# Expert biases as one-pass bf16 products in three parts, and expert 30's gate and up weights in single pieces

## The reference, cut to what matters

```
logits = xt @ router_w + router_b            # top 4 of 32, softmax gates
for each expert e, over its rows xb:
    gu  = xb @ w_gate_up[e] + b_gate_up[e]   # 1024 x 2048, bias 2048
    g, u = min(gu[:, :1024], 7), clip(gu[:, 1024:], -7, 7)
    act = (u + 1) * g * sigmoid(1.702 * g)
    y  += gate * (act @ w_down[e] + b_down[e])   # 1024 x 1024, bias 1024
```

## Time and profile before

| what | value |
|---|---|
| three runs | 1134.79, 1135.81 and 1138.35 us |
| the profiled execution: its time | 1133.35 us |
| the profiled execution: its span | 1131.5 us |
| mean granted clock of TensorE | 0.989 |
| read from HBM | 430.56 MB, 381 GB/s over the span |
| busy TensorE, DVE, ACT, GpSimd | 1089.5, 273.1, 156.6, 8.2 us |

### The profile page before, as it was taken

The page is one execution under the profiler, slowest core; times in us unless marked ns, Lnnn a source line. Parts: engine busy times, 40 slices in busy tenths (PEclk is TensorE's granted clock), DMA queues, the critical chain, the costliest instruction groups (busy, mean ns, idle before and its releaser), DMA issues.

```text
span 1131.5 us, 15121 instructions
## 1 busy us (share of the span) xinstructions
PE 1089.5 (96%) x6391; PEld 482.1 (43%) x6391; DVE 273.1 (24%) x701; ACT 156.6 (14%) x326; POOL 8.2 (1%) x20
## 2 busy tenths in 40 slices
PE   8999999999999899998999989999899998999997
PEld 6788885633333333333333333333233332333332
DVE  1698742551111111111111111111011110111111
ACT  3453341400000000000000000000000000010011
POOL 1000000000000000000000000000000000000000
PEclk9999999999999999999999989999899999999999
DMA  9933289699999999999999999999999999999994
GB/s 285 333 106 114 78 289 372 241 428 428 429 429 430 425 429 429 430 430 427 430 431 430 429 429 432 431 428 429 427 431 431 429 426 428 431 430 428 425 426 185
DMA packets 46231, 432.72 MB, mean 382 GB/s; under 512 B 4244, under 2 KB 23007, under 8 KB 28367
## 3 DMA queue, kind: packets, MB, share of 16 engines
q1 hardware_dynamic: 45472, 431.03, 91.4%
q0 software_dynamic: 320, 0.43, 0.2%
q10 hardware_dynamic: 366, 0.15, 0.1%
HBM read 430.56 MB, written 1.05 MB: 381 GB/s over the span
## 4 chain that ended last, share of the span: by engine, by line
PE 88%; DMA 7%; issue 2%; DVE 1%; ACT 1%; SPq 0%; DVEq 0%; ACTq 0%
PE psum L872 37%; PE psum L908 19%; DMA arena<-in_w_gate_up 7%; PE psum L668 5%; PE psum L918 5%; PE psum L841 4%; PE psum L578 4%; PE psum L893 3%; PE psum L861 3%; PE psum L716 2%; PE psum L743 2%; PE psum L887 1%; PE psum L850 1%; PE psum L659 1%; PE psum L619 0%
## 5 line engine op out<-in xcount | busy, mean ns | idle before, releaser
L872 PE MATMUL psum<-arena 128*64 128x512 f32 x2048 | 457.4, 605 | 26.5 <-issue 22.3
L872 PEld LDWEIGHTS psum<-arena 128*64 128x64 f32 x2048 | 146.5, 139 | 332.4 <-issue 324.8
L908 PE MATMUL psum<-arena 128*64 128x512 f32 x1024 | 227.0, 596 | 0.0
L1510 DVE TENSOR_SCALAR arena<-psum 128x512 f32<-128x512 f32 x32 | 22.1, 691 | 737.9 <-PE psum L872 733.7
L908 PEld LDWEIGHTS psum<-arena 128*64 128x64 f32 x1024 | 70.7, 137 | 153.8 <-issue 153.8
L1189 ACT COPY arena<-psum 128x256 f32<-128x256 f32 x32 | 11.9, 372 | 546.0 <-PE psum L850 546.0
L918 PE MATMUL psum<-arena 64*128 64x512 f32 x256 | 63.6, 615 | 0.7 <-ACT arena L1202 0.7
L668 PE MATMUL psum<-arena 128*128 128x256 f32 x256 | 59.0, 381 | 0.3 <-ACT arena L1085 0.3
L1202 ACT COPY arena<-psum 128x512 f32<-128x512 f32 x32 | 18.7, 585 | 271.7 <-PE psum L908 271.7
L668 PEld LDWEIGHTS psum<-arena 128*128 128x128 f32 x256 | 47.8, 190 | 7.3 <-ACT arena L1085 0.5
L841 PE MATMUL psum<-arena 128*128 128x64 bf16 x1488 | 48.4, 193 | 2.2
(11 more groups left out here) (222 smaller groups left out, 537.6 us busy)
## 6 DMA issues: line engine op xcount, KB each, us to landing
arena<-in_w_gate_up SPq DMA_DIRECT2D x56, 4096.0 KB, 29.2
arena<-in_w_down SPq DMA_DIRECT2D x63, 2048.0 KB, 26.3
arena<-in_w_gate_up SPq DMA_DIRECT2D x16, 2048.0 KB, 12.8
arena<-in_w_in SPq DMA_DIRECT2D x9, 1024.0 KB, 6.2
arena<-in_w_in SPq DMA_DIRECT2D x8, 512.0 KB, 8.2
arena<-in_w_out SPq DMA_DIRECT2D x2, 2048.0 KB, 14.0
arena<-in_x SPq DMA_DIRECT2D x4, 512.0 KB, 16.9
arena<-in_w_o_mla SPq DMA_DIRECT2D x1, 2048.0 KB, 11.4
```

What stands on the lines that cost most here:

```text
L872: last = mm(b[64 * half:64 * half + 64, :], xe[i][:, k, :], slot_gu[slot][:, j, o + half * 512:o + half * 512 + 512], start=(k == 0 and fi ...
L908: last = mm(b[64 * c:64 * c + 64, :], aT[:, j, 64 * h:64 * h + 64], slot_dn[slot][:, j, c * 512:(c + 1) * 512], start=False, stop=(h == DC ...
L1510: ts(g_s, G, LIMIT, None, ALU.min).then_inc(S.g_ready, 1)
```

## The change

The biases are stored as three bf16 parts whose sum is the float32 value: the rounded value, the rounded rest, and the rest of that. The three parts lie on three groups of 32 partitions (`PARTS` = 96), `pick` becomes a bf16 matrix that repeats the selection in each group, and one bf16 matmul over 96 partitions gives the selected bias. `biases` and `down_bias` become 4 and 2 such matmuls.

SP loads b_gate_up and b_down three times, on the three groups, into `staged`, which lies in the place of ring slot 3, when all gate columns are done; these six DMAs stand ahead of w_out. GpSimd makes the parts in 15 steps (`bias_step`): three copies to bf16 on 96 partitions, then twice three subtractions and three copies, on 64 and on 32 partitions. Piece 3, which goes into the slot of `staged`, is loaded after pieces 4 to 7 and after the 15th step. TensorE waits for that step before expert 0's biases; DVE waits only for the norm's weight.

Expert 30's gate and up pieces are no longer paired: four DMAs of 2 MB, and TensorE waits for each. For this TensorE's last round of five experts is written out behind a loop of five rounds. DVE's `hot` moves to another tile.

```diff
 E = 32
+BIAS_STEPS = 15
 TOPK = 4
...
 def in_pairs(n, c):
-    return c < GC and 2 < n < E - 1
+    return c < GC and 2 < n < E - 2
 def loads_of():
...
         at += D
-        biasgu = words(at, FF); at += FF
+        bias_gu = words(at, FF).bitcast(BF16); at += FF
         ov_s = words(at, 320)
...
         ph = [half_words(at), half_words(WB + 5120), half_words(at + 64)]; at += 128
-        pick = [words(at, 64), words(WB + 5184, 64), rwt[:, 0:2, :].rearrange("p k e -> p (k e)"),
-                rwt[:, 2:4, :].rearrange("p k e -> p (k e)"), words(at + 64, 64)]; at += 128
+        pick = [words(at + 32 * i, 32).bitcast(BF16) for i in range(ROUND - 1)] + [words(WB + 5184, 32).bitcast(BF16)]; at += 128
         xe = [grid(at, KD, SLOTS), grid(WB + 5504, KD, SLOTS), grid(at + 512, KD, SLOTS)]; at += 1024
...
         router_bias = tk[:, 384:384 + E]
+        bias_dn = [words(W0 + C_MASK, 256).bitcast(BF16), tk[:, 128:384].bitcast(BF16)]
+        PARTS = 3 * E
+        staged = words(slot_at[3], 3 * D)
         xn3 = words(WB, 3072).bitcast(BF16).rearrange("p (t s d) -> p t s d", t=2, s=3)
...
         in_wqb, in_wkvb, in_wo, in_pw2 = sem("in_wqb"), sem("in_wkvb"), sem("in_wo"), sem("in_pw2")
+        in_norm = sem("in_norm")
         in_wout, in_res, in_router, in_bias = sem("in_wout"), sem("in_res"), sem("in_router"), sem("in_bias")
...
                      "router_ready logits_ready bound_ready exp_done mask_ready rank_ready place_ready "
-                     "hi_ready remains_ready mid_ready split_ready cnt_ready gate_ready overflow_ready used built gathered "
+                     "hi_ready remains_ready mid_ready split_ready cnt_ready gate_ready overflow_ready bias_step used built gathered "
                      "xe_half xe_ready turned sT_ready g_ready a_step sg_ready act_ready aT_done aT_ready y_ready scattered0 scattered "
...
             load_piece(1)
+            sp.wait_ge(*piece_used["g", 7])
+            for i in range(3):
+                sp.dma_start(staged[E * i:E * (i + 1), 0:2 * FF], a["b_gate_up"][0]).then_inc(in_bias, 16)
+                sp.dma_start(staged[E * i:E * (i + 1), 2 * FF:3 * FF], a["b_down"][0]).then_inc(in_bias, 16)
             sp.wait_ge(S.oT_ready, 4)
...
             sp.dma_start(router_bias, a["router_b"][0].partition_broadcast(P)).then_inc(in_router, 16)
-            for k in (2, 3):
-                load_piece(k)
+            load_piece(2)
             sp.wait_ge(S.ymix_ready, 4)
...
                 load_piece(k)
+            sp.wait_ge(S.bias_step, BIAS_STEPS)
+            load_piece(3)
             for k in (8, 9):
...
             pool.wait_ge(S.oT_ready, 4)
-            for o in range(2):
-                pool.dma_start(biasgu[E * o:E * (o + 1), :], a["b_gate_up"][0][:, FF * o:FF * (o + 1)]
-                               ).then_inc(in_bias, 16)
-                pool.dma_start(biasgu[E * (2 + o):E * (3 + o), 0:512], a["b_down"][0][:, 512 * o:512 * (o + 1)]
-                               ).then_inc(in_bias, 16)
             with nc.allow_non_contiguous_dma(reason="the norm's weight in the order of the experts' rows"):
                 pool.dma_start(fnw.rearrange("p (c j) -> p c j", j=4),
-                               a["ffn_norm_w"][0].rearrange("(c p j) -> p c j", c=2, j=4)).then_inc(in_bias, 16)
+                               a["ffn_norm_w"][0].rearrange("(c p j) -> p c j", c=2, j=4)).then_inc(in_norm, 16)
+
+            pool.wait_ge(in_bias, 16 * 6)
+            parts = [(bias_gu, 0, 2 * FF), (bias_dn[0], 2 * FF, 512), (bias_dn[1], 2 * FF + 512, 512)]
+            done = 0
+            for level in range(3):
+                rows_in = slice(0, E * (3 - level))
+                for to, at, n in parts:
+                    y = staged[rows_in, at:at + n]
+                    if level:
+                        nc.gpsimd.tensor_tensor(y, y, to[rows_in, :], ALU.subtract).then_inc(S.bias_step, 1)
+                        done += 1
+                if level:
+                    pool.wait_ge(S.bias_step, done)
+                for to, at, n in parts:
+                    nc.gpsimd.tensor_copy(to[rows_in, :], staged[rows_in, at:at + n]).then_inc(S.bias_step, 1)
+                    done += 1
+                pool.wait_ge(S.bias_step, done)
+            assert done == BIAS_STEPS
         @block.tensor
...
                     for o, b in ((0, G), (1, U)):
-                        last = mm(b[64 * half:64 * half + 64, :], pick[p][E * o:E * (o + 1), :],
-                                  biasgu[E * o:E * (o + 1), half * 512:half * 512 + 512], start=first, stop=not first)
+                        at = o * FF + half * 512
+                        last = mm(b[64 * half:64 * half + 64, :], pick[p][0:PARTS, :], bias_gu[0:PARTS, at:at + 512],
+                                  start=first, stop=not first)
                 return last
...
                 for c in range(2):
-                    rows_of = slice(E * (2 + c), E * (3 + c))
-                    mm(b[64 * c:64 * c + 64, :], pick[p][rows_of, :], biasgu[rows_of, 0:512], start=True, stop=False)
+                    mm(b[64 * c:64 * c + 64, :], pick[p][0:PARTS, :], bias_dn[c][0:PARTS, :], start=True, stop=False)
             def down(n, p, pieces, halves=range(DC), b=Y, in_pieces=False):
...
                     pe.wait_ge(S.built, 1)
-                    pe.wait_ge(in_bias, 80)
+                    pe.wait_ge(S.bias_step, BIAS_STEPS)
                     last = biases(0, ROUND - 1, False)
...
             biases(1, 0, True)
-            with pe.Fori(0, (E - 2) // ROUND) as it:
+
+            def expert(n, u, gu, dn):
+                after = SIDE[(u + 1) % ROUND]
+                gate_up(n, SIDE[u], gu)
+                turn(n, SIDE[u])
+                turn_act(n - 1)
+                gather(n + 1, after)
+                down(n - 1, (u - 1) % ROUND, dn)
+                biases(n + 1, (u + 1) % ROUND, True)
+                scatter(n - 1, SIDE[u - 1])
+
+            rounds = (E - 2) // ROUND
+            with pe.Fori(0, rounds - 1) as it:
                 for u in range(ROUND):
-                    n, after = ROUND * it + (1 + u), SIDE[(u + 1) % ROUND]
-                    gate_up(n, SIDE[u], gu_of(1 + u, it))
-                    turn(n, SIDE[u])
-                    turn_act(n - 1)
-                    gather(n + 1, after)
-                    down(n - 1, (u - 1) % ROUND, dn_of(u, it))
-                    biases(n + 1, (u + 1) % ROUND, True)
-                    scatter(n - 1, SIDE[u - 1])
+                    expert(ROUND * it + (1 + u), u, gu_of(1 + u, it), dn_of(u, it))
+            for u in range(ROUND):
+                n = ROUND * (rounds - 1) + 1 + u
+                expert(n, u, gu_of(n), dn_of(n - 1))
             turn_act(E - 2)
...
             sum4, inv4, bound = tk[:, 120:122], tk[:, 122:124], tk[:, 124:126]
-            hot = tk[:, 128:256].rearrange("p (k e) -> p k e", k=TOPK)
+            hot = wp[0][:, 0, :].rearrange("p (k e) -> p k e", k=TOPK)
             def out_part(i):
...
             gates(0)
-            dve.wait_ge(in_bias, 80)
+            dve.wait_ge(in_norm, 16)
             dve.wait_ge(S.gathered, 1)
...
```

## The result

The kernel after takes 1125.2 us (median of six runs, 1123.8 to 1127.44), beside 1135.74 us for the kernel before: a ratio of 0.9914, 95% interval 0.9898 to 0.9931. That is 10.5 us by the medians and 9.8 by the ratio. The prediction said 1134.3 us, 1129.5 to 1139.0, and so missed the time by 9 us and its range by 4. The profiled executions took 1133.35 us before and 1127.44 us after.

A forecast was written before the change was run, and what follows sets the result against it. The prediction took the DMA engines' weight stream as the bound. On the profiled 1133.35 us, tail -2.05, start -0.3 and DVE delay +0.8 gave 1131.8; carrying -1.55 to the median gave 1134.3 us, range 1129.5 to 1139.0.

The forecast's parts named there:

- the middle term of the sum: From piece 10's issue at 218.0, 182 pieces load at the DMA engines' rate, 429 GB/s; no change in rate counted.
- the prediction's own signs of being wrong: Loop above 429 GB/s; pieces 3, 8, 9 landing after 218; piece 10's issue to the end changing by over 3 us.
- the stream gets denser: Rival, chance 0.12: earlier releases and smaller pieces even out the engines' last 10 us, winning 4.8 us more: 1129.5.
- TensorE as the bound: Rival, chance 0.03: TensorE sets the end, so all 40 us shed from the biases are gained: 1095.8.
- the late split: Rival, chance 0.06: GpSimd's split of the biases ends after about 208 and delays the stream; at the upper rate 1185.
- the shared port: Rival, chance 0.09: DVE waits for whole GpSimd instructions at two places, deciding from 5.8 us before 218; up to 1140.0.
- Tail, -2.05: After the last weight loads: 1.3 us until piece 189's landing limits it, plus 0.75 from the last down bias.
- Biases' price: On TensorE, 0.52 us per gate and up bias and 0.26 per down bias; 40 us less work over 32 experts.
- Six DMAs and piece 3 behind the split: Ahead of the stream: bias loads take 2 us to issue, 2.75 to move; they and the later piece 3 cost nothing.
- The split, 27 us from 149 to 176: GpSimd's 15 steps before the stream, taken at twice the memset's rate; bounds 14.4 to 105 us; 27 us of cover.
- DVE beside the split, +0.8: Before 218.0, two DVE instructions reading two SBUF tensors wait for GpSimd: 1.35 us less 0.55 slack; bounds 0 to 6.5.
- Start of the stream: Expert 0's shorter bias releases slots from piece 13 on earlier, closing part of a hole: 0.3 us won, bounds 0 to 0.5.

The follow-up runs named there:

- the one with the holds: Kernel before with TensorE's loop at the start of a block and eleven spare matmuls at each round's end: 1153.75 us, ratio 1.0167.
- the biases alone with the hint: Kernel before with the three-part bf16 biases and a back-edge prefetch hint on TensorE's loop, expert 30's pieces still paired: 1126.0 us, ratio 0.9925.
- The kernel after with its loop at 200: Kernel after with only TensorE's loop moved, to start at instruction 200 of a block of 256: 1132.31 us, ratio 0.9981.
- the kernel after run again: Kernel after, unchanged, measured again beside its variants: 1125.05 us, ratio 0.9917.
- the hint: Kernel before with only a back-edge hint (`hint_back_edge=True`) added to TensorE's loop: 1124.98 us, ratio 0.9912.
- the moved loop: Kernel before with only TensorE's loop moved, to start at instruction 0 of a block of 256: 1127.02 us, ratio 0.992.
- at 100: Kernel before with only TensorE's loop moved, to start at instruction 100 of a block of 256: 1134.7 us, ratio 1.0006.

## Why the prediction was wrong, step by step

**What bounds the kernel: right.** In all kernels but the one with the holds TensorE waits for weights up to the tail, and in all but one of these starts on piece 189 within 1.6 us of its landing (the biases alone with the hint: 2.5). TensorE shed 29.7 us of work and 22.3 us of stalls, and its waits for gate and up rows grew from 4.3 to 41.2 us.

**The step that failed.** It is the middle term of the sum, "then 182 pieces at the DMA engines' rate". Its change was put at nothing without a reason, with the rate carried over from 260 to 650 us of the kernel before, and it measured -7.7 us: the rate itself holds the fetches. What led to it stands in the part on expert 30's pieces: "Undoing the loop's last round costs nothing that I see", and of the stall at the loop end, that it "lies before a wait for data anyway". I had the stall before me and asked only what TensorE loses by it. I did not ask what TensorE's sequencer does in it. The fetches and the branches answer it: it loads instructions, over the DMA engines that the whole prediction had called the bound, in every round, 9 times 16 KB. Two of the prediction's own signs of being wrong came: the loop runs at 431 GB/s, and the distance from piece 10's issue to the end changed by 9.9 us, where 3 was the limit.

**The rival "the stream gets denser"** had the right place and came near in size (1129.5, chance 0.12). The effect that it names is real: the last 10 us of the stream went from a share of 0.52 to 0.88, 3.6 of the 4.8 us that it offered. But the cause is another. Moving the loop alone brings it (0.82), and the smaller pieces alone don't (0.49). What was argued against it, that with full queues each engine is fed all the time already, is true from 260 to 650 us (a share of 1.00 in both kernels) and says nothing of how evenly the engines end. Of the others, TensorE as the bound would have given 40 us; the late split did not come (174.2 against 203), and DVE's delay beside GpSimd was 1.0 us, where the shared port needed 5.8. A lower clock behind a wait just ahead of the tail shows in one profile, that of the biases alone with the hint (0.81).

**The sum without the fetches was right.** The kernel after with its loop at 200 has all that I costed and nothing of what I missed: 1132.31 beside 1134.49, -2.2 us (-1.2 between the profiled executions), where the sum said -1.55. By terms:

- *Tail, -2.05:* measured -2.2 in the kernel after and -2.2 in the one at 200 (23.3 to 21.1), -1.8 in the kernel after run again. Right, as was its limit: TensorE waits for piece 189.
- *Biases' price:* 4 instructions take 0.60 us with the last one's end, 0.53 until the next group (229.97 to 230.50 in the kernel after run again), where I took 0.52; the two of line 915 take 0.34 in the tail (1105.99 to 1106.33), where I took 0.26 (before: 1.0). In the loop and the tail the scatter behind the four then waits 0.26 us for ScalarE (31 waits, 8.3 us, in the second fence of waits), so there they cost 0.86 instead of 1.02; that hand-over I had missed. TensorE's busy time fell by 29.7 us and not by 40: by these prices 36.8 (1.15 an expert), and line 895's matmuls ran 7.7 us longer (465.1 against 457.4).
- *Six DMAs and piece 3 behind the split:* covered, as predicted. In the kernel after w_out lands at 161.4, pieces 3, 8 and 9 at 198.0, 204.4 and 215.1, and no wait of TensorE for them shows.
- *The split, 27 us from 149 to 176:* measured 149.36 to 174.22, in five groups:

```profile
149.36 3.65 POOL L550 CAST arena<-arena 96x2048 bf16<-96x2048 f32 x3 [3.41 <-DMA arena<-in_b_down]
153.10 7.28 POOL L545 TENSOR_TENSOR arena<-arena 64x2048 f32<-64x2048 f32 x3
160.44 3.00 POOL L550 CAST arena<-arena 64x2048 bf16<-64x2048 f32 x3
163.52 7.18 POOL L545 TENSOR_TENSOR arena<-arena 32x2048 f32<-32x2048 f32 x3
170.76 3.46 POOL L550 CAST arena<-arena 32x2048 bf16<-32x2048 f32 x3
```

A subtraction over 2048 columns took 4.06 us, a cast 1.88.
- *DVE beside the split, +0.8:* measured 1.0 us. In the kernel after run again the mixing's matmuls begin 0.38 us later than before and end 1.38 later (175.08 against 173.70). The waits of TensorE are where they were expected, at the two hand-overs (in the profiled kernel after):

```profile
152.60 0.70 PE L748 MATMUL psum<-arena 128*128 128x256 f32 x2 [0.41 <-DVE arena L1418]
...
160.46 3.91 PE L738 MATMUL psum<-arena 128*128 128x256 f32 x17 [0.26 <-issue]
```

DVE's own instructions show the cause. Lines 1417 and 1438 (before: 1387 and 1408) in the kernel after run again; before they took 0.68 and 1.23 us:

```profile
150.29 2.24 DVE L1417 TENSOR_TENSOR arena<-arena 128x512 f32<-128x512 f32 x1
...
153.20 0.68 DVE L1428 TENSOR_TENSOR arena<-psum,arena 128x512 f32<-128x512 f32 x1
...
156.76 2.22 DVE L1438 TENSOR_TENSOR arena<-arena 128x1024 f32<-128x1024 f32 x1
```

There GpSimd's first copy runs from 150.10 for 1.88 us, and its first subtraction from 153.83 for 4.06 us. The two DVE instructions end 0.55 and 1.09 us after these, about what they take alone. Line 1428, with one input in PSUM, took 0.68 beside GpSimd as it did without. The two instructions were held 1.56 and 0.99 us, behind a copy of 1.88 us and the last part of a subtraction, and TensorE lost 1.0. No run before this one shows the forecast's term of 0.8, which was an estimate; these two holds are what stands in its place. DVE's waits for whole GpSimd instructions, on which the third rival rests, are there, and its worst alignment did not come. That a shared port makes them is not shown.
- *Start of the stream:* piece 10 is issued at 219.36 in the kernel after run again, 1.4 us later than before, where 0.5 was forecast: 1.0 is DVE's, 0.4 was there before the mixing began, and nothing is seen of the 0.3 to be won. In the profiled execution after it comes 2.5 us later still (221.88), by a granted clock of 0.50 from 213 to 218; from 206 to 213 it was 0.90, with TensorE busy 6.70 of these 7 us. The kernel after run again has 1.00 in both. What makes it is open.

**The gain, added up.** Fetches: 8.8 us by moving the loop of before, 8.9 by the hint, 7.3 by moving the loop of after (ratios 0.9917 and 0.9981, times 1135.7). The rest of the change: 2.2 us, by the kernel at 200. 7.3 to 8.9 and 2.2 make 9.5 to 11.1; measured 9.8 to 10.5, and 8.8 to 9.4 in the kernel after run again. On top of the hint the parts of the change bring nothing that can be seen (1126.0 and 1125.64 against 1124.98), so that their 2.2 us add to the hint's 8.9 is not shown.

**Was it the change?** The biases' edit took 60 instructions out of the loop's body and 16 out of the code ahead of it, and with that the loop came to touch seven blocks. A body of 1740 fits seven blocks of 256 from 53 of 256 places (0 to 52), one of 1680 from 113. So the change made it likelier, and by this count an unrelated edit ahead of the loop could have won or lost as much. The loop of after at 200 is fetched again, so the shorter loop alone doesn't do it; most of the gain hangs on the place.

**What the fetches and the branch cost.** The branches back over 1680 instructions took 208 ns in the median with no fetch (the kernel after), and so did those over 1740 (the loop of before at 0); with nine fetches a round they took 6188. Before, the fetches cost 7 to 9 us in 1136 (by the moved loops and the hint).

## What to carry to other kernels

Where the DMA engines are the bound, read the line of instruction fetches on the page first (63 before, 24 after), and the duration of the branch that closes a long loop: here 6 us instead of 0.2 went with a body that was loaded again in each round, by the engines that are full. Try a hint for the back edge or another place of the loop before shortening anything: here the hint gave, in one line, what the whole change gave, and the other place 8.8 us of its 9.8 to 10.5. Compare the ends of two streams over the last microseconds before the last byte, not over the same clock times. And when two kernels differ in instruction count, compare each with its loop at a fixed place, or the placement (here 8.8 and 7.3 us) is measured instead of the change.

## What the runs showed of the hardware that I had not expected

A loop of 1740 instructions costs 1127.0 us or 1134.7 depending on where it starts (at 0 or at 100). A fetch of 16 KB cost the stream 2.6 times its bytes (1.51 MB less moved for 0.57 MB fetched, the moved loop against before), and the engines' uneven end cost about as much again (a share of 0.52 instead of 0.82 in the last 10 us). A hint for the back edge took away the last fetch of the first round (363 us before) and all later ones of the loop (none from 343 to 1080 us). DVE's instructions with two inputs in SBUF waited until GpSimd's running instruction had ended (2.24 instead of 0.68 us, and 2.22 instead of 1.23), the one with an input in PSUM did not (0.68 in both). A ring of ten slots of 2.1 MB hid 31 us of TensorE's time without a packet less in the stream. After waits of about 2.5 us TensorE ran some groups of 32 matmuls in 8.78 instead of 7.09 us, at a granted clock of 0.81 in the one shown, while others behind such waits took 7.09 us and the moved loop, whose longest wait for gate and up rows was 1.7 us, ran at a granted clock of 1.0 throughout. Written-out code is fetched as well: seven times between 940 and 1100 us, where the loop of the hinted kernel was fetched once.
